# The two rope query tiles computed in the joined stage instead of the latent stage

## The chip, the cores and the metric

The kernel runs on one core of one Trainium2 chip. The metric is the device time of the whole program in microseconds (us), the median of several executions. One launch computes both layers for a prompt of 1024 tokens and for 8 samples of 16 tokens each, 1152 token columns in all.

## The reference

Every layer projects the normalised rows by `w_in` and splits the columns among four head groups. Only one of them, the latent attention (MLA), is touched here:

```
def _rope(x, pos):
    ...
    return jnp.concatenate([x1 * cos - x2 * sin, x2 * cos + x1 * sin], axis=-1)

def _mla(xq, xlat, xkr, pos, past_lat, past_kr, lat_g, w_uk, w_uv):
    q = xq.reshape(B, L, MLA_H, MLA_DN + MLA_DR)          # 4 heads, 64 + 32
    q = jnp.concatenate([q[..., :MLA_DN], _rope(q[..., MLA_DN:], pos)], axis=-1)
    lat = _rmsnorm(xlat, lat_g)
    kr = _rope(xkr, pos)
    ...
    scale = (MLA_DN + MLA_DR) ** -0.5
```

Beside it run a differential attention (4 heads with two score maps each), a gated chunk mixer (SGU) and a gated delta rule (GDN) whose inputs pass through a causal convolution of width 4.

## The kernel before

All arrays lie transposed, features on the 128 partitions and tokens along the row, in 3 blocks of 384 columns. A projection tile is 128 output features: 8 pieces of the contraction by 3 blocks. Operands are kept as a high and a low part, so one piece of one block is three matmuls with 384 columns (lines 264 to 266, `split_product`); this is called an item. A tile has 24 items. The weights of a tile are loaded by SP (`w_load`), rounded by ACT (`w_high`, line 251) and completed by POOL (`w_low`, line 259, a subtraction that reads and writes SBUF). Tiles are numbered through a layer, `GDN_W` to `MLA_W` and on, and three split slots turn round by this number.

A layer is a row of stages; at the end of each stage all engines meet. Those that matter here, in their order:

- `diff_stage`: queries and keys of the differential attention.
- `diff_gdn_stage`, the joined stage: the differential attention (32 turns: two head pairs, 8 query blocks `i` of 128 rows, two heads `e`) and dense projection items are woven on each engine by one list written out by hand, `fill`, which says how many items come after each step of the attention. A turn of block `i` works on `128*(i+1)` keys. On PE a turn holds its scores (line 1262), the transposes of the weights (line 1272, which wait for the DVE result of line 1352) and the values (line 1284). On DVE a turn is two bias additions and two maxima (lines 1339 and 1340), then after ACT's exponents lines 1349 to 1352. The first six of the dense tiles are GDN inputs, and their convolution runs on DVE: one multiplication (line 1378) and three multiply-adds (line 1380) over 1176 columns, at fixed places of the item count; below this is called a burst. Tiles 6 and 7 are the GDN gates, the last two (`JOIN_TILES = GDN_TILES + 2`) the MLA queries without position. These four are copied by ACT to `row` and kept in device memory by SP (line 1178).
- `sgu_stage`: the chunk mixer; it also loads the kept queries into `qT`.
- `mla_stage`, the latent stage: four tiles in the order `MLA_ORDER = (4, 5, 2, 3)`, that is the latent (LAT), the rope key (KR), the rope query (QR) and the same with its halves swapped (QS). ACT squares the latent, PE sums the squares (line 459), DVE and ACT turn the sums into a factor (lines 527 to 530), DVE ropes the key (lines 516 to 519) and the query (lines 534 to 543). SP writes the key and the latent row to the outputs and waits until both have landed before the stage can end.
- `expand_stage`: keys and values are expanded from the latent row by PE, ACT, DVE and POOL (line 786 on). Then comes the latent attention.

Of the kernel before, what the change touches and what calls it, by code (L numbers as in the profile page):

```python
# [11 lines left out]
P = 128  # L12
# [65 lines left out]
EARLY = 3  # L78
DQK_W, DV_AT, GDN_W, SV_AT, SU_AT, MLA_W, OUT_W, FFN_W = 0, 4, 6, 16, 18, 20, 24, 32
MLA_ORDER = (4, 5, 2, 3)  # L80
MLA_LATE = len(MLA_ORDER)
JOIN_TILES = GDN_TILES + 2
DIFF_ORDER = (2, 3, 0, 1)
# [19 lines left out]
def build(nc, d):  # L103
    top = ExitStack()
    with top:
# [63 lines left out]
        gate_keep = nc.dram_tensor("gate_keep", (P, 2, TOK), F32, kind="Internal").ap()  # L169
        qn_keep = nc.dram_tensor("qn_keep", (P, 2, TOK), F32, kind="Internal").ap()  # L170
        y_keep = nc.dram_tensor("y_keep", (P, 6, TOK), F32, kind="Internal").ap()
# [133 lines left out]
        def sgu_stage(l):  # L305
# [9 lines left out]
            with stage("sgu_par", "prod_ready", "freed_a", "sv_ready", "sv_freed", "vn_ready", "mix_ready", "mix_done",  # L315
# [3 lines left out]
                @block.sync  # L319
                def _(sp):  # L320
                    sp.dma_start(wsT[:, :, :, :], d["sgu_wT"][l]).then_inc(spar, 16)
                    sp.dma_start(ln[:, :, :], d["sgu_ln"][l]).then_inc(spar, 16)
                    sp.dma_start(sb[:, :, :, :], d["sgu_b"][l]).then_inc(spar, 16)
                    for n in range(SV_AT + 4, MLA_W + 4):
                        w_load(sp, l, n)
                    for hh in range(HEADS):
                        sp.dma_start(qT[0:64, hh, :], qn_keep[64 * (hh % 2):64 * (hh % 2) + 64, hh // 2, :]).then_inc(qnin, 16)
# [94 lines left out]
        def mla_stage(l):  # L422

            cosT = at("cosT", [P, TOK], R(24))
            sinT = at("sinT", [P, TOK], R(25))
            t1 = at("rope_t1", [P, NB, BLK], R(26))
            sq = at("lat_sq", [P, NB, BLK], R(27))
            tk = at("rope_tk", [64, BLK], R(35))
            LAT, KR, QR, QS = 0, 1, 2, 3
            own = lambda n: "V" if n in (KR, QR, QS) else "A"  # L430
            with stage("mla_aux", "prod_ready", "freed_a", "freed_v", "lat_sq_ready", "lat_sum", "lat_ready", "kr_ready",
                       "mla_link", "kv_out", "lat_recip", "lat_root") as (block, sems):
                (aux, ready, fa, fv, lsq, lsum, lready, krready, lnk, kvout, lrc, lrt) = sems
                freed = {"A": fa, "V": fv}

                @block.sync
                def _(sp):
                    for dst, src in ((cosT, "cos"), (sinT, "sin")):
                        sp.dma_start(dst[:, :], d[src]).then_inc(aux, 16)
                    for dst, src in ((wuk, "wuk"), (wuv, "wuv")):  # L440
                        sp.dma_start(dst[:, :], d[src][l]).then_inc(aux, 16)
# [21 lines left out]
                def _(pe):  # L463
                    for n in range(MLA_LATE):
                        pe.wait_ge(w_lod, MLA_W + n + 1)
                        slot = (MLA_W + n) % SSLOTS
                        for b in range(NB):
                            u = n * NB + b
                            cols = slice(b * BLK, (b + 1) * BLK)
                            if u >= 6:  # L470
                                who = own((u - 6) // NB)
                                pe.wait_ge(freed[who], sum(own(v // NB) == who for v in range(u - 5)))
                            for k in range(KD):
# [4 lines left out]
                        if n == KR:  # L478
                            lat_sums(pe, range(2))
                        if n == QR:  # L480
                            lat_sums(pe, range(2, NB))

# [6 lines left out]
                def _(act):  # L489
# [10 lines left out]
                    split(1)  # L500
                    split(2)
                    for b in range(NB):
                        if b == 2:
                            split(3)
                        act.wait_ge(lrc, b + 1)
                        act.sqrt(PS[:, 6 + b % 2, 0:BLK], PS[:, 6 + b % 2, 0:BLK]).then_inc(lrt, 1)

                @block.vector
                def _(dve):
                    scale = (MLA_DN + MLA_DR) ** -0.5  # L510
                    link = Link(dve, lnk)
                    dve.wait_ge(aux, 80)
                    for b in range(NB):
                        cols = slice(b * BLK, (b + 1) * BLK)
# [7 lines left out]
                    for b in range(NB):  # L522
# [14 lines left out]
                    for b in range(NB):  # L537
                        dve.wait_ge(ready, QS * NB + b + 1)
                        link(dve.scalar_tensor_tensor(out=bank(QS, b), in0=bank(QS, b), scalar=scale,
                                                      in1=sinT[:, b * BLK:(b + 1) * BLK], op0=ALU.mult,  # L540
                                                      op1=ALU.mult))
                        for hh in range(HEADS):
                            ins = dve.tensor_tensor(qT[64:96, hh, b * BLK:(b + 1) * BLK],
                                                    t1[32 * hh:32 * hh + 32, b, :],
                                                    bank(QS, b)[32 * hh:32 * hh + 32], ALU.add)
                        ins.then_inc(fv, 1)

# [548 lines left out]
        def diff_gdn_stage(l, bias):  # L1096
# [47 lines left out]
            with stage(*names) as (block, sems):  # L1144
# [4 lines left out]
                def _(sp):  # L1149
# [13 lines left out]
                    def projection():  # L1163
                        for t in range(ITEMS):
# [26 lines left out]
                    sp.wait_ge(acc_kept, 32 * 6)  # L1191
                    sp.wait_ge(row_kept[0], 32)
                    sp.wait_ge(row_kept[1], 32)

# [196 lines left out]
                def _(act):  # L1391
# [41 lines left out]
                    def projection():  # L1433
                        for t in range(ITEMS):
# [4 lines left out]
                            if j == 0 and 0 <= u < JOIN_TILES * NB:  # L1439
# [4 lines left out]
                                if b == 0 and n >= GDN_TILES:  # L1444
                                    act.wait_ge(row_kept[n % 2], 16)
# [1551 lines left out]
```

## Time and profile before

| what | value |
|---|---|
| median of 3 runs | 3513.42 us (3512.93 to 3527.26) |
| profiled execution, first to last instruction | 3513.3 us |
| PE busy | 3245.8 us (92%) |
| DVE busy | 2026.6 us (58%) |
| ACT busy | 902.5 us (26%) |
| POOL busy | 893.2 us (25%) |
| mean granted TensorE clock | 0.959 of 2.4 GHz |

The profiled execution is listed by its span, 3513.3 us; no other time of it is given, and the span lies 0.1 us under the median. A matmul's busy time counts its way through the array, so a PE that is shown busy is not a PE at its peak. The stages named above take, in the first layer, 134.8 to 348.8 us (joined), 348.8 to 412.1 (chunk mixer), 412.1 to 468.4 (latent) and 468.4 to 480.1 us (expand); the second layer repeats them 1725 us later.

### The profile page before, as it was taken

Reading aid. Unit: us, or ns where it says so; the run is one execution under the profiler, and the core shown is the slowest. Engines: PE = TensorE matmul, PEld = TensorE weight load, DVE = VectorE, ACT = ScalarE, POOL = GpSimd, SP = SyncE. Lnnn points to the kernel's source line nnn. Section 1 sums busy time; section 2 is a strip of 40 time slices with the busy share of each in tenths; the row PEclk is TensorE's granted clock in tenths of the full one; section 3 lists DMA queues with packets and bytes.
Section 4 is the critical chain, followed back from the end, with each engine's and each line's share of the span. In section 5 each row is a group of like instructions: output and inputs, shape, how many; then the busy total and the mean of one; then the engine's idle time right before and its main releaser. Section 6 shows DMA issues by size and latency. Waiting matters only on the chain. (4 is left out here: it accounts for less than half of the span.)

```text
span 3513.3 us, 57203 instructions
## 1 busy us (share of the span) xinstructions
PE 3245.8 (92%) x23900; PEld 3044.1 (87%) x23900; DVE 2026.6 (58%) x3500; ACT 902.5 (26%) x1650; POOL 893.2 (25%) x780
## 2 busy tenths in 40 slices
PE   5989988889999999999988999979899999999996
PEld 4978975779999999999978898648699999999996
DVE  7386454564555565555566755546627655555656
ACT  3244134233211111111233431532322111111112
POOL 2222120213322222222343211102133222222223
PEclk9999998799999999999999999979899999999998
DMA  5622231201111111111154212230011111111112
GB/s 211 194 88 95 90 115 41 82 18 37 41 43 43 43 42 37 49 37 43 35 179 151 94 70 91 95 115 9 23 43 41 49 37 37 49 43 43 42 43 71
DMA packets 122292, 237.42 MB, mean 68 GB/s; under 512 B 34084, under 2 KB 82980, under 8 KB 118632
## 3 DMA queue, kind: packets, MB, share of 16 engines
q1 hardware_dynamic: 122024, 233.65, 20.4%
q8 instruction: 192, 3.15, 0.4%
q14 instruction: 76, 0.62, 0.1%
HBM read 176.70 MB, written 56.54 MB: 66 GB/s over the span
## 5 line engine op out<-in xcount | busy, mean ns | idle before, releaser
L264 PE MATMUL PS<-h_split,w_split 128*128 128x384 f32 x3072 | 1064.9, 347 | 28.2 <-PEq L201 14.1
L266 PE MATMUL PS<-h_split,w_split 128*128 128x384 f32 x3072 | 1044.4, 340 | 0.0
L265 PE MATMUL PS<-h_split,w_split 128*128 128x384 f32 x3072 | 1040.1, 339 | 0.0
L259 POOL TENSOR_TENSOR w_split<-w_full,w_split 128x1024 fp32r<-128x1024 f32 (+1 forms) x194 | 476.6, 2457 | 963.5 <-ACT w_split L251 963.5
L264 PEld LDWEIGHTS PS<-h_split,w_split 128*128 128x128 f32 x3072 | 586.3, 191 | 47.5 <-issue 29.3
L265 PEld LDWEIGHTS PS<-h_split,w_split 128*128 128x128 f32 x3072 | 582.8, 190 | 2.5
L266 PEld LDWEIGHTS PS<-h_split,w_split 128*128 128x128 f32 x3072 | 582.3, 190 | 0.0
L251 ACT CAST w_split<-w_full 128x1024 fp32r<-128x1024 f32 (+1 forms) x194 | 202.0, 1053 | 1306.1 <-PE PS L266 1167.1
L2296 DVE TENSOR_TENSOR x<-x,PS 128x384 f32<-128x384 f32 x528 | 285.6, 552 | 178.5 <-PE PS L266 176.8
L264 PE MATMUL PS<-ffn_act,w_split 128*128 128x384 f32 x1056 | 367.7, 348 | 8.1 <-POOL w_split L259 7.1
L265 PE MATMUL PS<-ffn_act,w_split 128*128 128x384 f32 x1056 | 357.1, 338 | 0.0
L266 PE MATMUL PS<-ffn_act,w_split 128*128 128x384 f32 x1056 | 356.7, 338 | 0.0
L264 PEld LDWEIGHTS PS<-ffn_act,w_split 128*128 128x128 f32 x1056 | 199.4, 189 | 28.8 <-DVE x L2296 20.3
L2246 DVE TENSOR_TENSOR ffn_row<-PS,square_sums 128x384 f32<-128x384 f32 x176 | 93.3, 551 | 207.9 <-PE PS L266 205.6
L265 PEld LDWEIGHTS PS<-ffn_act,w_split 128*128 128x128 f32 x1056 | 199.5, 189 | 0.5
L266 PEld LDWEIGHTS PS<-ffn_act,w_split 128*128 128x128 f32 x1056 | 199.2, 189 | 0.0
L2267 DVE SCALAR_TENSOR_TENSOR ffn_gate<-ffn_row,par,ffn_gate 128x584 f32<-128x584 f32 x176 | 175.1, 1019 | 1.8
L2250 DVE TENSOR_TENSOR ffn_row<-PS,square_sums 128x256 f32<-128x256 f32 x88 | 37.4, 425 | 235.2 <-PE PS L266 235.2
L2267 DVE SCALAR_TENSOR_TENSOR ffn_up<-ffn_row,par,ffn_up 128x584 f32<-128x584 f32 x176 | 141.4, 843 | 3.0
L264 PE MATMUL PS<-o_hi,w_split 128*128 128x384 f32 x384 | 132.5, 345 | 10.7 <-DVE o_lo L1980 10.7
L2152 POOL COPY ffn_new<-ffn_row 128x2 f32<-128x2 f32 x88 | 17.5, 199 | 477.5 <-DVE ffn_row L2251 477.4
L1411 ACT ACTIVATE diff_P<-PS,diff_stat 128x128 f32<-128x128 f32 (+7 forms) x128 | 95.8, 748 | 148.3 <-DVE diff_stat L1340 148.2
(388 smaller groups left out, 4920.4 us busy)
## 6 DMA issues: line engine op xcount, KB each, us to landing
w_full<-in_w_up SPq DMA_DIRECT2D x88, 512.0 KB, 3.3
w_full<-in_w_down SPq DMA_DIRECT2D x44, 512.0 KB, 3.3
w_full<-in_w_in SPq DMA_DIRECT2D x38, 512.0 KB, 3.4
kq_keep<-split_rows SPq DMA_DIRECT2D x128, 128.0 KB, 2.4
kq_row<-kq_keep SPq DMA_DIRECT2D x32, 512.0 KB, 4.3
x<-x_keep SPq DMA_DIRECT2D x2, 4608.0 KB, 16.9
w_full<-in_w_out SPq DMA_DIRECT2D x16, 512.0 KB, 3.3
gdn_y<-y_keep SPq DMA_DIRECT2D x2, 3456.0 KB, 11.7
```

Source lines behind the costliest of these rows:

```text
L251: act.copy(ws[:, n % SSLOTS, 0, 0:w], wf[:, n % WSLOTS, 0:w]).then_inc(w_hid, 1)
L259: pool.tensor_tensor(ws[:, n % SSLOTS, 1, 0:w], wf[:, n % WSLOTS, 0:w], ws[:, n % SSLOTS, 0, 0:w].bitcast(F32), ALU.subtract).then_inc(w_l ...
L264: pe.matmul(out, w_hi, a_hi, start=first, stop=False)
L265: pe.matmul(out, w_hi, a_lo, start=False, stop=False)
L266: return pe.matmul(out, w_lo, a_hi, start=False, stop=last)
L1411: act.activation(Pb[:, v % 2, c, 0:n], S(c)[:, 0:n], ACT.Exp, bias=stat[:, 0, v, c:c + 1], accum_out=stat[:, 1, v, c:c + 1]).then_inc(p_do ...
L2152: pool.tensor_copy(new[:, t, 0:pad], row[:, SEQ:SEQ + pad])
L2246: dve.tensor_tensor(row[:, pad + b * BLK:pad + (b + 1) * BLK], src, ss[:, b, :], ALU.mult).then_inc(upf, 1)
L2250: dve.tensor_tensor(row[:, pad + 2 * BLK:pad + SEQ], src[:, 0:rest], ss[:, b, 0:rest], ALU.mult)
L2267: ins = dve.scalar_tensor_tensor(out=acc[:, a:b], in0=row[:, tap + a:tap + b], scalar=w(tap), in1=acc[:, a:b], op0=ALU.mult, op1=ALU.add)
L2296: dve.tensor_tensor(xs, xs, PS[:, 4 + u % 4, 0:BLK], ALU.add).then_inc(added, 1)
```

## The change

QR and QS leave the latent stage and become dense tiles 10 and 11 of the joined stage. There ACT scales and copies them like the other query tiles, and SP keeps all four in `q_keep`. The lists of the weave grow: the 16 turns of blocks 0 to 3 carry 9 items instead of 7, the 16 turns of blocks 4 to 7 carry 8 instead of 7, and 14 items remain behind the last turn as before. The latent stage loads the two kept rows into `rope_rows` behind cos and sin; DVE ropes the query from there before it touches the key. The swapping of weights into slots keeps its order, with the numbers of the tiles between moved by two.

```diff
-DQK_W, DV_AT, GDN_W, SV_AT, SU_AT, MLA_W, OUT_W, FFN_W = 0, 4, 6, 16, 18, 20, 24, 32
-MLA_ORDER = (4, 5, 2, 3)
+DQK_W, DV_AT, GDN_W, SV_AT, SU_AT, MLA_W, OUT_W, FFN_W = 0, 4, 6, 18, 20, 22, 24, 32
+MLA_ORDER = (4, 5)
-JOIN_TILES = GDN_TILES + 2
+JOIN_TILES = GDN_TILES + 4
...
+            qr = at("rope_rows", [P, 2, TOK], R(28))
...
                     for dst, src in ((cosT, "cos"), (sinT, "sin")):
                         sp.dma_start(dst[:, :], d[src]).then_inc(aux, 16)
+                    sp.dma_start(qr[:, :, :], q_keep[:, 2:4, :]).then_inc(rin, 16)
...
                         if n == KR:
-                            lat_sums(pe, range(2))
-                        if n == QR:
-                            lat_sums(pe, range(2, NB))
+                            lat_sums(pe, range(NB))
...
                     dve.wait_ge(aux, 80)
+                    dve.wait_ge(rin, 16)
+                    for b in range(NB):
+                        cols = slice(b * BLK, (b + 1) * BLK)
+                        dve.tensor_tensor(t1[:, b, :], qr[:, 0, cols], cosT[:, cols], ALU.mult)
+                        link(dve.tensor_tensor(qr[:, 1, cols], qr[:, 1, cols], sinT[:, cols], ALU.mult))
+                        for hh in range(HEADS):
+                            rows = slice(32 * hh, 32 * hh + 32)
+                            dve.tensor_tensor(qT[64:96, hh, cols], t1[rows, b, :], qr[rows, 1, cols], ALU.add)
...
-                    for b in range(NB):
-                        dve.wait_ge(ready, QR * NB + b + 1)
-                        dve.scalar_tensor_tensor(out=t1[:, b, :], in0=bank(QR, b), scalar=scale,
-                                                 in1=cosT[:, b * BLK:(b + 1) * BLK], op0=ALU.mult,
-                                                 op1=ALU.mult).then_inc(fv, 1)
...
-                fill += [3, 2, 2] if i < 4 else [2, 2, 2, 1]
+                fill += [3, 3, 3] if i < 4 else [2, 2, 2, 2]
...
-                                dst = gate_keep[:, n - 6, :] if n < GDN_TILES else qn_keep[:, n - GDN_TILES, :]
+                                dst = gate_keep[:, n - 6, :] if n < GDN_TILES else q_keep[:, n - GDN_TILES, :]
```

DVE in the joined stage, first head pair, the turn of query block 3 whose weights are 128x512 (`diff_P` is the weight row, `conv_acc` the convolution's sum). Before:

```order
L1352 SCALAR_TENSOR_TENSOR diff_P<-diff_P,diff_stat 128x512
L1339 TENSOR_TENSOR PS<-PS,bias_p_245 128x256
L1340 TENSOR_REDUCE diff_stat<-PS 128x1
L1339 TENSOR_TENSOR PS<-PS,bias_p_245 128x256
L1340 TENSOR_REDUCE diff_stat<-PS 128x1
L1349 RECIPROCAL diff_stat<-diff_stat 128x1
L1350 TENSOR_SCALAR diff_stat<-diff_stat,lam 128x1
L1352 SCALAR_TENSOR_TENSOR diff_P<-diff_P,diff_stat 128x512
```

The same place of the changed kernel:

```order
L1336 SCALAR_TENSOR_TENSOR diff_P<-diff_P,diff_stat 128x512
L1323 TENSOR_TENSOR PS<-PS,bias_p_245 128x256
L1324 TENSOR_REDUCE diff_stat<-PS 128x1
L1323 TENSOR_TENSOR PS<-PS,bias_p_245 128x256
L1324 TENSOR_REDUCE diff_stat<-PS 128x1
L1362 TENSOR_SCALAR conv_acc<-conv_row,par 128x1176
L1364 SCALAR_TENSOR_TENSOR conv_acc<-conv_row,par,conv_acc 128x1176 x3
L1333 RECIPROCAL diff_stat<-diff_stat 128x1
L1334 TENSOR_SCALAR diff_stat<-diff_stat,lam 128x1
L1336 SCALAR_TENSOR_TENSOR diff_P<-diff_P,diff_stat 128x512
```

The bursts stand at fixed item counts, so with more items in a turn they come in earlier turns. Before, one of the six fell whole into a turn (the first of block 4) and five were cut in two; now four fall whole into a turn (the first of block 3, the second of block 4, the first of block 6, the second of block 7) and two are cut.

DVE in the latent stage. Before, its last rows of the stage: the third block's norm, then the query's rope.

```order
L527 TENSOR_SCALAR PS<-PS 128x384
L528 RECIPROCAL PS<-PS 128x384
L530 SCALAR_TENSOR_TENSOR latT<-latT,par,PS 128x384
L534 SCALAR_TENSOR_TENSOR rope_t_4556<-PS,cosT 128x384 x3
L539 SCALAR_TENSOR_TENSOR PS<-PS,sinT 128x384
L543 TENSOR_TENSOR qT<-rope_t_4556,PS 32x384 x4
```

Now the query's rope opens the stage, three times the first three of these rows, and the key's rope follows; the norm rows come last:

```order
L507 TENSOR_TENSOR rope_t_4747<-rope_rows,cosT 128x384
L508 TENSOR_TENSOR rope_rows<-rope_rows,sinT 128x384
L511 TENSOR_TENSOR qT<-rope_t_4747,rope_rows 32x384 x4
L515 TENSOR_TENSOR rope_tk<-PS,cosT 32x384
L516 TENSOR_TENSOR rope_tk<-PS,sinT 32x384
L517 COPY PS<-rope_tk 32x384
L518 TENSOR_TENSOR krT<-rope_tk,PS 32x384
```

Moved ahead are 3 times 6 instructions, which now read SBUF alone where they read PSUM. PE at the end of the key tile, before:

```order
L264 MATMUL PS<-h_split,w_split 128x384
L265 MATMUL PS<-h_split,w_split 128x384
L266 MATMUL PS<-h_split,w_split 128x384
L459 MATMUL PS<-lat_sq,ones 128x384 x2
L264 MATMUL PS<-h_split,w_split 128x384
L265 MATMUL PS<-h_split,w_split 128x384
L266 MATMUL PS<-h_split,w_split 128x384
```

And now (line 740 is the first product of the expand stage):

```order
L264 MATMUL PS<-h_split,w_split 128x384
L265 MATMUL PS<-h_split,w_split 128x384
L266 MATMUL PS<-h_split,w_split 128x384
L459 MATMUL PS<-lat_sq,ones 128x384 x3
L207 UNCONDITIONAL_BRANCH
L736 UNCONDITIONAL_BRANCH
L740 MATMUL PS<-latT,wuk 128x512 x4
```

The 144 matmuls of QR and QS no longer stand between the sums and the end of the stage.

## Rows read from the trace of the kernel before

**Rows 1.** Timeline of one layer, SP and POOL: start us, us, engine, line, operation.
```profile
134.78 0.34 SPq L1181 DMA_DIRECT2D conv_old<-in_c_gconv  x1
...
348.81 0.35 SPq L321 DMA_DIRECT2D wsT<-in_sgu_wT  x1
...
412.11 0.35 SPq L439 DMA_DIRECT2D cosT<-in_cos  x1
...
468.43 2.01 POOL L786 COPY kT<-krT 32x1024 f32<-32x1024 f32 x2 [13.26 <-SPq L207]
...
480.14 0.54 SPq L2755 DMA_DIRECT2D o_diff<-dqT  x1
```

**Rows 2.** Timeline of PE in the latent stage: starts 18 items apart.
```profile
454.72 0.35 PE L264 MATMUL PS<-h_split,w_split 128*128 128x384 f32 x1
...
464.20 0.35 PE L264 MATMUL PS<-h_split,w_split 128*128 128x384 f32 x1
```

**Rows 3.** Groups of the joined stage, 137:347: busy, mean ns, idle before.
```profile
L1262 PE MATMUL PS<-k_stack,q_stack 128*128 128x512 f32 (+3 forms) x96 | 28.3, 351 | 4.4 <-POOL q_stack L567 2.6 <-ACT diff_P L1411 1.6
...
L1272 PE MATMUL PS<-cst,diff_P 128*128 128x128 f32 x144 | 25.0, 284 | 13.8 <-DVE diff_P L1352 9.2 <-ACT diff_PT_odd L1398 3.0 <-ACT diff_PT_even L1398 1.5
...
L1272 PEld LDWEIGHTS PS<-cst,diff_P 128*128 128x128 f32 x144 | 17.8, 144 | 19.9 <-DVE diff_P L1352 12.1 <-issue 7.0
```

**Rows 4.** Timeline of PE's weight loads in the joined stage, two long stalls.
```profile
203.74 0.71 PEld L1272 LDWEIGHTS PS<-cst,diff_P 128*128 128x128 f32 x4 [4.55 <-DVE diff_P L1352]
...
279.27 0.19 PEld L1262 LDWEIGHTS PS<-k_stack,q_stack 128*128 128x128 f32 x1 [2.91 <-POOL q_stack L567]
```

**Rows 5.** Timeline of DVE around a whole convolution burst.
```profile
191.95 0.88 DVE L1352 SCALAR_TENSOR_TENSOR diff_P<-diff_P,diff_stat 128x640 f32<-128x640 f32 x1
...
196.01 6.37 DVE L1380 SCALAR_TENSOR_TENSOR conv_acc<-conv_row,par,conv_acc 128x1176 f32<-128x1176 f32 x3
...
202.80 0.88 DVE L1352 SCALAR_TENSOR_TENSOR diff_P<-diff_P,diff_stat 128x640 f32<-128x640 f32 x1
```

**Rows 6.** Timeline of POOL and DVE: one operation beside POOL's and alone.
```profile
158.39 3.48 POOL L259 TENSOR_TENSOR w_split<-w_full,w_split 128x1024 fp32r<-128x1024 f32 x1
...
160.20 1.95 DVE L1352 SCALAR_TENSOR_TENSOR diff_P<-diff_P,diff_stat 128x256 f32<-128x256 f32 x1
...
165.51 0.49 DVE L1352 SCALAR_TENSOR_TENSOR diff_P<-diff_P,diff_stat 128x256 f32<-128x256 f32 x1
```

**Rows 7.** Windows: us, busy (x) of PE, PEld, DVE, ACT, POOL, PEclk, DMA.
```profile
200.00:210.00 10.00, 6.26 (x23) 5.80 (x24) 8.66 (x13) 3.00 (x7) 2.34 (x3) 0.66 0.53 164
```

**Rows 8.** Timeline of DVE in the latent stage.
```profile
437.71 0.55 DVE L516 TENSOR_TENSOR rope_tk<-PS,cosT 32x384 f32<-32x384 f32 x1 [1.94 <-PE PS L266]
...
440.31 0.57 DVE L527 TENSOR_SCALAR PS<-PS 128x384 f32<-128x384 f32 x1 [0.32 <-DVE krT L519]
...
452.29 0.57 DVE L527 TENSOR_SCALAR PS<-PS 128x384 f32<-128x384 f32 x1 [3.42 <-PE PS L459]
...
456.00 0.62 DVE L530 SCALAR_TENSOR_TENSOR latT<-latT,par,PS 128x384 f32<-128x384 f32 x1 [0.54 <-ACT PS L506]
...
465.53 2.25 DVE L543 TENSOR_TENSOR qT<-rope_t,PS 32x384 f32<-32x384 f32 x4
```

**Rows 9.** Groups of DVE in the latent stage, 411:469.
```profile
L543 DVE TENSOR_TENSOR qT<-rope_t,PS 32x384 f32<-32x384 f32 x12 | 6.6, 552 | 0.2
```

**Rows 10.** Timeline of SP: the latent row's output.
```profile
456.78 0.37 SPq L449 DMA_DIRECT2D out_o_lat<-latT  x1
```

**Rows 11.** DMA issues: KB each, median us to landing.
```profile
qn_keep<-conv_row SPq DMA_DIRECT2D x1, 576.0 KB, 2.8
...
sgu_keep<-suT SPq DMA_DIRECT2D x1, 1152.0 KB, 6.3
```

**Rows 12.** Timeline of PE at the expand stage, first and second layer.
```profile
468.46 5.37 PE L756 MATMUL PS<-latT,wuk 128*128 128x512 f32 x8 [3.57 <-PEq L201]
...
2194.05 3.67 PE L756 MATMUL PS<-latT,wuk 128*128 128x512 f32 x8 [3.58 <-PEq L201]
```

More of the change, by code:

```diff
@@ L169, in build @@
         gate_keep = nc.dram_tensor("gate_keep", (P, 2, TOK), F32, kind="Internal").ap()
-        qn_keep = nc.dram_tensor("qn_keep", (P, 2, TOK), F32, kind="Internal").ap()
+        q_keep = nc.dram_tensor("q_keep", (P, 4, TOK), F32, kind="Internal").ap()
         y_keep = nc.dram_tensor("y_keep", (P, 6, TOK), F32, kind="Internal").ap()
@@ L326, in _ @@
                     for hh in range(HEADS):
-                        sp.dma_start(qT[0:64, hh, :], qn_keep[64 * (hh % 2):64 * (hh % 2) + 64, hh // 2, :]).then_inc(qnin, 16)
+                        sp.dma_start(qT[0:64, hh, :], q_keep[64 * (hh % 2):64 * (hh % 2) + 64, hh // 2, :]).then_inc(qnin, 16)
                     sp.wait_ge(vnr, TT)
@@ L428, in mla_stage @@
             tk = at("rope_tk", [64, BLK], R(35))
-            LAT, KR, QR, QS = 0, 1, 2, 3
-            own = lambda n: "V" if n in (KR, QR, QS) else "A"
+            LAT, KR = 0, 1
             with stage("mla_aux", "prod_ready", "freed_a", "freed_v", "lat_sq_ready", "lat_sum", "lat_ready", "kr_ready",
-                       "mla_link", "kv_out", "lat_recip", "lat_root") as (block, sems):
-                (aux, ready, fa, fv, lsq, lsum, lready, krready, lnk, kvout, lrc, lrt) = sems
-                freed = {"A": fa, "V": fv}
+                       "mla_link", "kv_out", "lat_recip", "lat_root", "rows_in") as (block, sems):
+                (aux, ready, fa, fv, lsq, lsum, lready, krready, lnk, kvout, lrc, lrt, rin) = sems
                 @block.sync
@@ L469, in _ @@
                             cols = slice(b * BLK, (b + 1) * BLK)
-                            if u >= 6:
-                                who = own((u - 6) // NB)
-                                pe.wait_ge(freed[who], sum(own(v // NB) == who for v in range(u - 5)))
                             for k in range(KD):
@@ L500, in _ @@
                     split(1)
-                    split(2)
                     for b in range(NB):
-                        if b == 2:
-                            split(3)
                         act.wait_ge(lrc, b + 1)
@@ L509, in _ @@
                 def _(dve):
-                    scale = (MLA_DN + MLA_DR) ** -0.5
                     link = Link(dve, lnk)
                     dve.wait_ge(aux, 80)
+                    dve.wait_ge(rin, 16)
[6 more added lines that the diff above has]
+                            dve.tensor_tensor(qT[64:96, hh, cols], t1[rows, b, :], qr[rows, 1, cols], ALU.add)
                     for b in range(NB):
@@ L531, in _ @@
                                                  in1=s, op0=ALU.mult, op1=ALU.mult).then_inc(lready, 1)
-                    for b in range(NB):
-                        dve.wait_ge(ready, QR * NB + b + 1)
-                        dve.scalar_tensor_tensor(out=t1[:, b, :], in0=bank(QR, b), scalar=scale,
-                                                 in1=cosT[:, b * BLK:(b + 1) * BLK], op0=ALU.mult,
-                                                 op1=ALU.mult).then_inc(fv, 1)
[L537 to L546, printed above, removed]
         def keep_stacked(sp, n, halves, done):
@@ L1191, in _ @@
                     sp.wait_ge(acc_kept, 32 * 6)
-                    sp.wait_ge(row_kept[0], 32)
-                    sp.wait_ge(row_kept[1], 32)
+                    sp.wait_ge(row_kept[0], 16 * (JOIN_TILES - 6) // 2)
+                    sp.wait_ge(row_kept[1], 16 * (JOIN_TILES - 6) // 2)
                 @block.gpsimd
@@ L1444, in projection @@
                                 if b == 0 and n >= GDN_TILES:
-                                    act.wait_ge(row_kept[n % 2], 16)
+                                    act.wait_ge(row_kept[n % 2], 16 * ((n - 6) // 2))
                                 elif b == 0 and n >= 2:
```

## The prediction

> **What bounds the kernel now.** The page comes first: PE is busy for 92% of the span, so what counts is where PE is held up and what of its work can slide under somebody else's wait. The timeline of SP gives the stages [rows 1]: the joined stage lasts 348.81 - 134.78 = 214.0 us, the latent stage 468.43 - 412.11 = 56.3 us, the expand stage 480.14 - 468.43 = 11.7 us. The second layer repeats them, so every sum below is made for one layer and doubled.
>
> The groups of the joined stage show PE's idle time: 13.8 us ahead of the transposes, most of it until DVE's weight row (line 1352), and 4.4 us ahead of the scores, 18.2 us in all [rows 3]. Seen from the weight loads, 12.1 us in nine waits are for DVE [rows 3]. The longest, 4.55 us [rows 4], stands behind the one convolution burst that lies whole in a turn: from one weight row to the next DVE needs 202.80 - 191.95 = 10.85 us there, without a pause worth naming [rows 5]. After that wait the granted clock of the slice is 0.66 [rows 7], that is 6.8 of 10 us at 1.2 GHz, for 3.4 us of lost work. The next long wait, 2.91 us, is for POOL's copy of keys and queries, whose load SP had issued late [rows 4].
>
> The latent stage has dense matmuls from its start to 464.6, and DVE's chains are hidden beneath them: the key's rope (to about 440.0), the norm of blocks 0 and 1 and, after a wait of 3.42 us for PE's late sum, of block 2 (to 456.6) [rows 8]. The output of the latent row is issued at 456.78 [rows 10] and has 11 us to land before DVE ends at 467.8 [rows 8], so it costs nothing.
>
> **The change part by part.**
>
> *Work added to the joined stage.* 18 items take 464.20 - 454.72 = 9.48 us, 0.527 us each [rows 2]. Two tiles are 48 items: +25.3 us if nothing hides them.
>
> *What hides them.* Each turn now holds 1.05 us (blocks 0 to 3) or 0.53 us (blocks 4 to 7) more of PE's work, so each wait for DVE shrinks by that much, if DVE's share of the turn stays as it was. It doesn't quite: four bursts now lie whole in a turn instead of one. PE's mean turn was (214 - 32 items outside the turns x 0.527) / 32 = 6.2 us, and is 0.5 to 1.1 us longer now; DVE's burst turn is 10.85 us at block 4, less where rows are shorter, and DVE has some 2 us of lead to spend. That makes 2.3 us of wait at block 3, 3 us at block 4 (4.55 - 0.53 with POOL's subtraction in it, 2 without), 2 us at block 6, none at the second of block 7 (short rows follow), 0.8 us at the two cut ones. That is 8.1 instead of 12.1 us, -4.0. The wait for POOL's copy goes, since it came from SP standing behind a late burst and the bursts are now over before: -2.9. Waits for ACT's copies between transposes (4.5 us of the 13.8) have as many items between them as before and stay; for the small rest -1.0. One of two clock drops goes: half of 3.4, -1.7. The joined stage thus grows by 25.3 - 4.0 - 2.9 - 1.0 - 1.7 = **+15.7 us**. Bounds: all 18.2 us of idle time and the 3.4 us of clock come back, +3.7; nothing comes back, +25.3.
>
> The rest that moves there lies beside PE's 25 us: on SP two weight loads and two keeps, on ACT two casts and six copies, on POOL two subtractions (2.4 us each when alone). ACT and POOL are busy for a quarter of the span, so none is counted; if SP is late with a key load through them, it costs PE the 2.91 us of [rows 4] again, which a rival below takes up.
>
> *Work taken from the latent stage.* PE ends the key tile at 437.7, as before (DVE's first row behind it starts at 437.71 [rows 8]). Only the chain is left. DVE starts later than it could: it waits for cos, sin, the kept rows and three small loads, 2.75 MB. Before, the same number of bytes had landed with `sgu_keep`, issued at 416.4 and down 6.3 us later [rows 11], at 422.7; I take 422.3. The query's rope is 18 operations of about 0.552 us [rows 9] plus links, 10.3 us. In it falls POOL's subtraction at 427 (2.4 us). The rows show what that can do: the same multiply-add took 1.95 us beside POOL's subtraction and 0.49 us alone, and ended when POOL's did [rows 6]. So 0 to 2.4 us are added, I take 1.6. The query's rope ends at 434.2; the key's three blocks (2.3 us each) end at 441.1 to 441.6 instead of 440.0, 1.5 us late. One block of the norm takes 456.62 - 452.29 = 4.3 us [rows 8]; the third no longer waits for PE and follows at once, so the latent row is done at 440.31 + 3 x 4.3 + 1.5 = 454.7. SP issues its output 0.2 us later, alone on the queue now: 2.8 us, as `qn_keep` of the same size [rows 11]. Then 0.7 us to the next stage's first work, as between 467.8 and 468.43 [rows 1, 8]: the stage ends at 458.4 instead of 468.4, **-10.0 us**. So of 25.3 us taken from PE 15 are not won, because a DVE chain and one landing come out from under it. Bounds: -11.6 (DVE never late) and -7 (loads down at 424.5 and a full hold).
>
> On DVE's hold the Trainium skill (SBUF — State Buffer, section on the two separate sides) says that a DVE operation with two SBUF inputs and a GpSimd operation that reads SBUF exclude each other for the whole instruction, whoever starts first. The old rope read PSUM and was free of it; the new one falls under it. By that rule the hold is either the rest of 2.4 us or, if DVE comes first, none for DVE, and my sum moves by -1.6 or +0.8 us a layer.
>
> *The expand stage.* PE idles for 20 us before it instead of 3.6. In the first layer its first eight rows took 5.37 us with a clock drop, in the second 3.67 us without [rows 12], and both stages last 11.7 us, since POOL sets the end. So one short drop is free; a longer one costs some: **+0.7 us**, from 0 to about 4.8, an estimate for the case that the 3.67 us and the products behind them, as many again, all run at half rate, less the time that POOL needs anyway.
>
> *Sum.* 15.7 - 10.0 + 0.7 = +6.4 us a layer, +12.8 us for both: 3513.3 + 12.8 = **3526 us**. The profiled span is within 0.1 us of the median, so no correction is needed. It is 0.4% slower, within 0.5%, which is about what a measurement of this kernel can tell from no change.
>
> **The rivals.**
>
> *The joined stage takes it all in.* If DVE's backlog clears, the bursts' waits vanish: +3.7 - 9.3 = -5.6 a layer, 3502 us. For it speaks that no burst is left for the second head pair, against it that a whole burst outlasts PE's turn by some 4 us. Faster by over 0.5% needs still more, joined growth under 0.5 us. Chance 0.12 for about 3502, half of it below 3496.
>
> *The bursts and SP cost as much as they free (slower).* Place: the turns of blocks 4 and 6. If two of the whole bursts each bring the 4.55 us seen at the one of before, with a clock drop of 3.4 us each, and SP's two more ordered waits make one load late again, the growth stays at 25 us: +25 - 9.3 = +15.7 a layer, 3545 us. It decides from a joined growth of 18.1 us on, where the total passes 0.5%. For it: DVE's 10.85 us against PE's 6.7 to 7.3. Chance 0.27.
>
> *The latent stage comes back colder and later.* Loads down at 424.5, a full hold and 4.8 us in the expand stage: 15.7 - 7 + 4.8 = 13.5 a layer, 3540 us. Chance 0.09. The Trainium skill (TensorE: Matmul & The Clock Gate, section on the clock gate) says that the throttled clock is the default and activity releases it; by that rule 20 us of idling makes the drop certain in both layers, where the rows show it in one of two. A certain short drop changes nothing in the sum.
>
> **How the numbers follow.** The forecast (3515 to 3536) has 0.52, the full intake 0.12, the busy bursts 0.27, the cold stage 0.09. Of the forecast's own share a fifth lies above 3531. Slower by over 0.5% (3531): 0.1 + 0.24 + 0.06 = about 0.38; faster 0.07; within 0.5% the rest, 0.55. The range from 3504 to 3545 leaves out some 0.08 below and 0.1 above.
>
> **What the changed profile would show.** The joined stage at about 230 us (218 or 239 by the rivals); waits for DVE of about 8 us, longest at blocks 3, 4 and 6; none for POOL's copy. In the latent stage DVE's rope from about 422, one of its rows stretched to some 2 us; PE idle for 20 us; the output of the latent row issued at about 42.7 us after the stage's start and landed 3 us later. I am wrong if the joined stage is off by more than 5 us, or if something other than this landing ends the latent stage.

## The result, and the profile after

| kernel | median, us | from to, us | runs | against before |
|---|---|---|---|---|
| before | 3516.13 | 3510.25 to 3527.26 | 22 | |
| changed | 3524.86 | 3516.8 to 3537.28 | 22 | 1.0022, 95% interval 1.0014 to 1.003 |

The change costs 0.22%, some 9 us, and lies within 0.5%. The forecast was 3526 us, +12.8 over its own base; its base of 3513.3 us lies 2.8 us under the median of the 22 runs. The stage boundaries on SP come first, as in [rows 1]; they are those of the changed kernel, first layer, and then the second layer's:

```profile
135.03 0.34 SPq L1165 DMA_DIRECT2D conv_old<-in_c_gconv  x1
...
361.11 0.35 SPq L321 DMA_DIRECT2D wsT<-in_sgu_wT  x1
...
424.43 0.35 SPq L438 DMA_DIRECT2D cosT<-in_cos  x1
...
472.21 2.99 POOL L770 COPY kT<-krT 32x1024 f32<-32x1024 f32 x3 [27.36 <-SPq L207]
...
484.16 0.54 SPq L2739 DMA_DIRECT2D o_diff<-dqT  x1
...
1864.20 0.34 SPq L1165 DMA_DIRECT2D conv_old<-in_c_gconv  x1
...
2089.71 0.35 SPq L321 DMA_DIRECT2D wsT<-in_sgu_wT  x1
...
2152.98 0.35 SPq L438 DMA_DIRECT2D cosT<-in_cos  x1
...
2202.20 5.33 PE L740 MATMUL PS<-latT,wuk 128*128 128x512 f32 x8 [10.49 <-PEq L201]
...
2213.88 0.53 SPq L2739 DMA_DIRECT2D o_diff<-dqT  x1
```

Of the kernel before, [rows 1] has the first layer; two more of its second layer are:

```profile
2136.15 0.35 SPq L439 DMA_DIRECT2D cosT<-in_cos  x1
...
2205.73 0.54 SPq L2755 DMA_DIRECT2D o_diff<-dqT  x1
```

Differences of these starts give the lengths (an expand stage ends with `o_diff`):

| stage, us | before, layers 1 and 2 | changed | difference |
|---|---|---|---|
| joined | 214.0, 212.1 | 226.1, 225.5 | +12.1, +13.4 |
| chunk mixer | 63.3, 63.3 | 63.3, 63.3 | 0 |
| latent | 56.3, 57.9 | 47.8, 49.2 | -8.5, -8.7 |
| expand | 11.7, 11.7 | 11.9, 11.7 | +0.2, 0 |

They sum to +8.5 us, the 8.7 us between the medians. The two profiled spans are further apart, 3526.5 and 3513.3: the 4.7 us more lie nearly all in stages that the change does not touch, behind the second expand stage (1312.6 us against 1307.6). In the profiles of the experiments below that same stretch takes 1304 to 1313 us, so stages are compared here, not spans. A stage too is not the same from profile to profile: four kernels below keep the joined stage of the changed kernel as it is, and there it takes 224.2 to 228.6 us, 226.3 in the mean of their eight. So the growth of the joined stage is known to some 2 us.

The groups of PE in the changed joined stage, 137:352, answer to [rows 3]; the columns are the same. The window ends before the last 8 of the 144 transposes; up to the end of the stage, the wait for DVE is the same 8.0 us:

```profile
L1246 PE MATMUL PS<-k_stack,q_stack 128*128 128x512 f32 (+3 forms) x96 | 27.4, 341 | 2.4 <-POOL q_stack L551 1.4 <-ACT diff_P L1395 1.1
L1256 PE MATMUL PS<-cst,diff_P 128*128 128x128 f32 x136 | 22.7, 274 | 9.4 <-DVE diff_P L1336 6.5 <-ACT diff_PT_odd L1382 1.7 <-ACT diff_PT_even L1382 1.2
...
L1256 PEld LDWEIGHTS PS<-cst,diff_P 128*128 128x128 f32 x136 | 16.8, 140 | 12.9 <-DVE diff_P L1336 8.0 <-issue 3.8
```

The weight loads' wait for DVE fell from 12.1 to 8.0 us in five waits. The longest of them, and the one for POOL's copy:

```profile
163.72 0.20 PEld L1256 LDWEIGHTS PS<-cst,diff_P 128*128 128x128 f32 x2 [1.22 <-DVE diff_P L1336]
...
194.40 0.42 PEld L1256 LDWEIGHTS PS<-cst,diff_P 128*128 128x128 f32 x4 [1.37 <-DVE diff_P L1336]
...
204.76 0.30 PEld L1246 LDWEIGHTS PS<-k_stack,q_stack 128*128 128x128 f32 x2 [1.68 <-POOL q_stack L551]
...
217.29 0.42 PEld L1256 LDWEIGHTS PS<-cst,diff_P 128*128 128x128 f32 x4 [2.89 <-DVE diff_P L1336]
...
239.82 0.42 PEld L1256 LDWEIGHTS PS<-cst,diff_P 128*128 128x128 f32 x4 [2.28 <-DVE diff_P L1336]
```

The whole joined stage as one window (us, busy and count of PE, PEld, DVE, ACT, POOL, granted clock), before and then changed, first and second layer each:

```profile
134.78:348.81 214.03, 192.77 (x1249) 176.11 (x1250) 150.86 (x249) 96.72 (x240) 59.31 (x62) 0.96 0.31 103
1860.77:2072.83 212.06, 192.00 (x1249) 176.14 (x1250) 148.84 (x249) 96.82 (x240) 59.50 (x62) 0.96 0.31 104
```

```profile
135.03:361.11 226.08, 211.11 (x1393) 198.20 (x1394) 152.25 (x249) 100.70 (x248) 64.95 (x64) 0.99 0.32 108
1864.20:2089.71 225.51, 211.51 (x1393) 198.47 (x1393) 152.23 (x249) 100.80 (x248) 65.03 (x64) 0.98 0.32 108
```

PE's idle time is the length less the busy time: 21.3 us before, 15.0 after, -6.3 (second layer 20.1 and 14.0). The time lost to the clock is estimated as the length times what the clock lacks to 1: 0.04 x 214 = 8.6 before, 0.01 x 226 = 2.3 after (second layer 8.5 and 4.5). The clock is given in hundredths, so each of these is good to about 1 us. The same sum over windows of 10 us gives 8.1 before and 2.7 after, and 8.5 and 3.5 in the second layer. Of these, 3.0 and 2.7 (1.7 and 1.7 in the second layer) are lost in the first 10 us of the stage, in both kernels.

DVE and POOL in the changed latent stage, against [rows 8]:

```profile
435.97 0.56 DVE L507 TENSOR_TENSOR rope_t<-rope_rows,cosT 128x384 f32<-128x384 f32 x1 [12.16 <-DMA wukT<-in_wukT]
...
442.61 2.66 DVE L507 TENSOR_TENSOR rope_t<-rope_rows,cosT 128x384 f32<-128x384 f32 x1
...
448.03 0.55 DVE L515 TENSOR_TENSOR rope_tk<-PS,cosT 32x384 f32<-32x384 f32 x1
...
455.65 0.57 DVE L526 TENSOR_SCALAR PS<-PS 128x384 f32<-128x384 f32 x1 [0.32 <-DVE krT L518]
...
467.83 0.61 DVE L529 SCALAR_TENSOR_TENSOR latT<-latT,par,PS 128x384 f32<-128x384 f32 x1 [0.54 <-ACT PS L498]
```

```profile
442.05 2.80 POOL L259 TENSOR_TENSOR w_split<-w_full,w_split 128x1024 fp32r<-128x1024 f32 x1 [14.11 <-ACT w_split L251]
```

DVE stands until the last small load has landed, 11.5 us into the stage (12.9 in the second layer), then works through without a gap worth naming to 468.44: query, key, norm. One query row began 0.56 us behind POOL's subtraction and ended 0.42 us behind it; it took 2.66 us instead of 0.56. The latent row's output is issued 44.2 us into the stage and the next stage begins 3.6 us after it.

### The profile page after: what moved, and what is told of

Same layout as the page of the kernel before. It is cut to its first block and busy times, and to the rows that moved or that the text cites. A ratio compares the mean times of both kernels' runs of the same rounds, so it can differ in the third digit from the quotient of the medians.

```text
span 3526.5 us, 57213 instructions
## 1 busy us (share of the span) xinstructions
PE 3245.1 (92%) x23900; PEld 3044.9 (86%) x23900; DVE 2034.9 (58%) x3500; ACT 906.3 (26%) x1662; POOL 894.2 (25%) x780
## 5 line engine op out<-in xcount | busy, mean ns | idle before, releaser
L259 POOL TENSOR_TENSOR w_split<-w_full,w_split 128x1024 fp32r<-128x1024 f32 x194 | 478.9, 2469 | 976.0 <-ACT w_split L251 976.0
L264 PEld LDWEIGHTS PS<-h_split,w_split 128*128 128x128 f32 x3072 | 584.3, 190 | 47.8 <-issue 29.8
L251 ACT CAST w_split<-w_full 128x1024 fp32r<-128x1024 f32 x194 | 201.9, 1052 | 1277.6 <-PE PS L266 1138.4
```

Of the source, the lines that this page charges most:

```text
L251: act.copy(ws[:, n % SSLOTS, 0, 0:w], wf[:, n % WSLOTS, 0:w]).then_inc(w_hid, 1)
L259: pool.tensor_tensor(ws[:, n % SSLOTS, 1, 0:w], wf[:, n % WSLOTS, 0:w], ws[:, n % SSLOTS, 0, 0:w].bitcast(F32), ALU.subtract).then_inc(w_l ...
L264: pe.matmul(out, w_hi, a_hi, start=first, stop=False)
```

## The experiments

Each ran beside the kernel before on one chip. Ratios are to that kernel, whose median there was 3519 to 3521 us and not 3516; so ratios are compared, and not times.

**All new items behind the last turn.**

```diff
-                fill += [3, 3, 3] if i < 4 else [2, 2, 2, 2]
+                fill += [3, 2, 2] if i < 4 else [2, 2, 2, 1]
```

> The changed kernel with the old weave (7 items in every turn), so that the 48 items of the two tiles stand behind the last turn. Theory: these items are worth their 25.3 us of PE a layer, and only their place inside the turns hides part of it. Then the joined stage lasts 214 + 25 = 239 us instead of 226, PE's waits for DVE are back at some 12 us in nine, and the program is about 25 us slower than the changed kernel, 3550 us, 1.0% over the kernel before. Rival: DVE bounds the joined stage, so that it doesn't matter where PE's items stand; then the stage stays at about 226 us and the program at 3525.

Measured: 3550.78 us, ratio 1.0089 (1.0061 to 1.0117). The joined stage takes 236.8 and 240.5 us, 10.7 and 14.9 more than in the changed kernel; the weight loads wait 10.7 us for DVE:

```profile
L1256 PEld LDWEIGHTS PS<-cst,diff_P 128*128 128x128 f32 x144 | 17.7, 142 | 18.2 <-DVE diff_P L1336 10.7 <-issue 6.6
```

Against the kernel before, the stage is 22.8 and 28.4 us longer, 25.6 in the mean. So the 25 us of items are full price where nothing covers them, and the places in the turns earn back about half. That is what the changed lists are worth.

**The bursts spread.** The four convolution operations of a tile stand 5 items apart instead of 2, the store of the result 7 items later.

```diff
-                            n, j = divmod(t - 36, TILE_ITEMS)
+                            n, j = divmod(t - 43, TILE_ITEMS)
...
-                            if 0 <= n < 6 and j % 2 == 0 and j // 2 < GDN_TAPS:
-                                j //= 2
+                            if 0 <= n < 6 and j % 5 == 0 and j // 5 < GDN_TAPS:
+                                j //= 5
```

> The changed kernel with the four convolution operations of a tile five items apart instead of two (and the output of its sum issued seven items later), so that none of the six bursts lies whole in a turn. Theory: the 8 us of waits for DVE's weight rows come from whole bursts; they fall to 2 to 3 us, the joined stage from 226 to about 220 us, the program by 8 to 12 us to about 3515, level with the kernel before. Rival: the waits come from the chain of exponents on ACT and would be there without bursts; then they stay at 8 us and nothing moves by more than 2 us.

Measured: 3504.62 us, ratio 0.9952 (0.9934 to 0.997). Groups of its joined stage, 137:352, and the stage as windows:

```profile
L1246 PE MATMUL PS<-k_stack,q_stack 128*128 128x512 f32 (+3 forms) x96 | 27.3, 340 | 2.0 <-ACT diff_P L1395 1.1 <-POOL q_stack L551 0.9
L1256 PE MATMUL PS<-cst,diff_P 128*128 128x128 f32 x144 | 23.6, 273 | 2.1 <-ACT diff_PT_odd L1382 1.3 <-ACT diff_PT_even L1382 0.8
```

```profile
134.74:351.61 216.87, 209.24 (x1393) 197.64 (x1394) 147.98 (x249) 101.01 (x248) 59.20 (x64) 0.99 0.33 112
1862.24:2078.36 216.12, 209.20 (x1393) 197.62 (x1394) 147.13 (x249) 101.01 (x248) 59.45 (x64) 0.99 0.33 112
```

No wait for DVE is left in the groups, with the same DVE work, and idle time falls from 15.0 to 7.6 us. The stage is 9.2 and 9.4 us shorter. This is the length that my rival of full intake named (+3.7 over before; measured +2.8 and +4.1). What had kept the change from it is the lump of the bursts and nothing about the amount of work. The gain is larger than expected (about 220 us and 3515). The store had to move with the operations; its own share is not separated here, but the weight loads' wait for POOL's copy fell only from 1.7 to 1.2 us. Three later kernels with the same spread have joined stages of 215.7 to 217.5 us.

**The same spread on the kernel before**, to tell whether the room came from the change.

> The kernel before, with its own lists of the weave and its latent stage of four tiles, and the four convolution operations of a tile spread over 5 items each instead of 2. Theory (the lump alone makes the waits): the 12.1 us of waits for DVE and the clock drops behind them go here as well, the joined stage shrinks from 214.0 and 212.1 to about 201, the program by about 24 us, to about 3493; moving the two tiles is then worth nothing by itself. Rival (the two moved tiles made the room in which the spread operations fit): with 7 items in a turn DVE is still late on average, some 6 us of waits stay, the joined stage is 207 or more and the program 3505 or more, no faster than the changed kernel with the same spread.

Measured: 3502.69 us, ratio 0.9946 (0.9931 to 0.9962); joined stage 202.5 and 203.9 us. Groups of its weight loads, 137:343:

```profile
L1272 PEld LDWEIGHTS PS<-cst,diff_P 128*128 128x128 f32 x144 | 17.7, 140 | 10.7 <-issue 5.8 <-DVE diff_P L1352 3.9
L1262 PEld LDWEIGHTS PS<-k_stack,q_stack 128*128 128x128 f32 x96 | 17.6, 188 | 8.1 <-POOL q_stack L567 6.6 <-ACT diff_P L1411 1.2 <-issue 0.3
```

It lies between the two theories: the joined stage nearer to the first (201), the program's time nearer to the rival (3505). The wait for DVE falls from 12.1 to 3.9 us, not to none, so the 7 items of a turn seem a little short; and the wait for POOL's copy grows from 2.9 to 6.6 us. Against the changed kernel with the same spread the joined stage is 14.4 and 12.2 us shorter and the latent and expand stages together 9.6 and 8.2 us longer: moving the tiles costs some 4 to 5 us a layer with or without the lump. That is read from the stages of one profile of each kernel; the ratios, 0.9946 and 0.9952, cannot tell it from nothing.

**SP's store asked for 3 items later**, on that kernel (`t - 46` instead of `t - 43`).

> The kernel before with the convolution operations spread over 5 items, and SP's store of a finished convolution row asked for 3 items later, so that SP doesn't stand behind DVE with a load of keys and queries queued after it. Theory (the 6.6 us of waits for POOL's copy that the spread brought come from SP waiting for the later last operation): they fall under 3 us, the joined stage goes from 202.5 and 203.9 to about 199, the program from 3502.7 to about 3495. Rival (the load is late by its own place in the order, or DVE then waits for the stored row): the joined stage stays at 202 or more and the program within 3 us of 3502.7.

Measured: 3501.47 us, ratio 0.9946 (0.9933 to 0.9959), joined stage 200.6 and 201.0 us. A row of its waits (who, for whom, us in all, times, the longest):

```profile
PEld PS L1262 <- POOL q_stack L567: 3.1, 1, 3.1
```

The wait for POOL's copy halves, and the stage shortens by 1.9 and 2.9 us, no more than a stage differs between profiles. SP standing behind DVE was half of that wait. The program's time stayed within 3 us of 3502.7, as the rival had it, and not at 3495; so the wait is explained, but its worth is not shown.

**The kept rows loaded in the chunk mixer**, so that DVE waits only for cos and sin.

```diff
+                    sp.dma_start(qr[:, :, :], q_keep[:, 2:4, :]).then_inc(qnin, 16)
                     sp.wait_ge(vnr, TT)
...
-                        sp.dma_start(dst[:, :], d[src]).then_inc(aux, 16)
-                    sp.dma_start(qr[:, :, :], q_keep[:, 2:4, :]).then_inc(rin, 16)
+                        sp.dma_start(dst[:, :], d[src]).then_inc(rin, 16)
...
-                    dve.wait_ge(aux, 80)
-                    dve.wait_ge(rin, 16)
+                    dve.wait_ge(rin, 32)
```

> The changed kernel with the kept query rows loaded during the chunk mixer stage into free rows, and DVE in the latent stage waiting for cos and sin alone instead of all five loads and the rows. Theory: DVE's late start (11.5 and 12.9 us into the stage) is what makes the latent stage's chain late; it starts at about 6 us, the key's rope ends right behind PE (27 to 28 us in), and the latent stage falls by 3 to 4 us a layer to about 44.5, the program by 6 to 8 us to about 3518. Rival: POOL's subtraction and PE's clock set the chain; then DVE starts earlier, waits for PE at the key and the stage falls by less than 1 us.

Measured: 3520.45 us, ratio 1.0003 (0.9989 to 1.0018). DVE in its second and in its first layer:

```profile
2159.52 0.56 DVE L506 TENSOR_TENSOR rope_t<-rope_rows,cosT 128x384 f32<-128x384 f32 x1 [7.95 <-DMA sinT<-in_sin]
```

```profile
444.91 0.55 DVE L514 TENSOR_TENSOR rope_tk<-PS,cosT 32x384 f32<-32x384 f32 x1 [2.86 <-PE PS L270]
...
449.12 0.55 DVE L514 TENSOR_TENSOR rope_tk<-PS,cosT 32x384 f32<-32x384 f32 x1 [1.94 <-PE PS L270]
```

DVE starts 7.3 us into the second layer's stage instead of 12.9, but the key's rope then waits for PE's key tile, and the latent stage gains 1.4 and 1.7 us only (46.4 and 47.5). It is between the theory (3 to 4 us) and the rival (under 1). The late loads were worth that much and no more: right behind them stands PE.

**The landing of the outputs awaited one stage later.** SP waits for both latent outputs in the expand stage (a semaphore `lat_out` that outlives the stage) instead of in the latent stage.

> The changed kernel in which the outputs of latent row and rope key are awaited at the end of the expand stage instead of the latent stage. Theory: the landing of the latent row ends the latent stage (3.6 us from its issue to the next stage, of which 0.7 us are the change of stages); the stage falls by 2.8 us a layer to 45, the program by some 5.5 us to 3519. Rival: PE's cold clock takes it back, since the expand stage begins 3 us sooner but lasts longer; then the expand stage grows by 2 us or more and less than 2 us are won in all.

Measured: 3520.54 us, ratio 1.0000 (0.9985 to 1.0015). PE's first row of the expand stage comes 45.7 us after the latent stage's start in both layers, against 47.8 and 49.2; output issue to next stage is now 1.3 us instead of 3.6:

```profile
468.94 0.37 SPq L449 DMA_DIRECT2D out_o_lat<-latT  x1
...
470.24 5.68 PE L743 MATMUL PS<-latT,wuk 128*128 128x512 f32 x8 [8.16 <-PEq L201]
```

So 2.3 us of the chain were the landing, a layer. The expand stage stays at 11.7 us, so the rival's slower clock takes nothing back.

**The norm first.** PE sums the squares of a block behind the next block, DVE makes the norm, then the key's rope, the query's last; the latent row's output is issued before the key's.

```diff
-                        if n == KR:
-                            lat_sums(pe, range(NB))
+                            if 1 <= u <= NB:
+                                lat_sums(pe, [u - 1])
```

> The changed kernel; in the latent stage the sums of squares follow each block, DVE makes the norm first, then the key's rope, and the query's rope last, so that the latent row's output lands under DVE's work. Theory (the stage's end is DVE's chain plus one landing): the 2.8 us of landing and the wait of 11.5 us before DVE's first row come out of the chain, the latent stage falls from 47.8 and 49.2 to about 42, the program by about 12 us, to about 3513. Rival (something else, PE or the other loads, ends the stage): it stays above 46 and the program at 3520 or more.

Measured: 3512.88 us, ratio 0.9982 (0.9972 to 0.9991). Timelines of DVE, and of SP and PE:

```profile
434.49 0.57 DVE L513 TENSOR_SCALAR PS<-PS 128x384 f32<-128x384 f32 x1 [11.56 <-PE PS L459]
...
456.00 0.56 DVE L531 TENSOR_TENSOR rope_t<-rope_rows,cosT 128x384 f32<-128x384 f32 x1 [0.24 <-DVE krT L526]
...
463.70 2.24 DVE L535 TENSOR_TENSOR qT<-rope_t,rope_rows 32x384 f32<-32x384 f32 x4
```

```profile
448.70 0.36 SPq L447 DMA_DIRECT2D out_o_lat<-latT  x1
...
466.61 6.63 PE L745 MATMUL PS<-latT,wuk 128*128 128x512 f32 x8 [14.01 <-PEq L201]
```

The latent stage is 466.61 - 423.55 = 43.1 us (44.1 in the second layer), 4.7 and 5.1 less. The output now lands under the query's rope, and the rope itself takes 9.9 us without a stretched row, since POOL's subtraction now falls elsewhere; so the gain holds both, the landing and some 2 us of that row. DVE still begins only 10.9 us into the stage, now for PE's first sum.

**Two blocks of the query's rope in the expand stage**, on top of that.

> As the one with the norm first, and blocks 1 and 2 of the query's rope move on DVE into the expand stage, where POOL sets the end. Theory: the latent stage is about 35 us, the expand stage 12 to 13, both together 48 instead of 59.7 and 60.9, the program by about 24 us less than the changed kernel, about 3501. Rival (DVE is late for its copies in the expand stage and that stage grows by what the other lost): both together 54 or more, the program 3512 or more.

Measured: 3504.26 us, ratio 0.9958 (0.9944 to 0.9972). DVE and PE in its expand stage:

```profile
458.86 1.42 DVE L768 TENSOR_TENSOR rope_t<-rope_rows,cosT 128x384 f32<-128x384 f32 x1 [0.68 <-PEq L205]
```

```profile
469.40 3.02 PE L750 MATMUL PS<-wuv,latT 128*128 128x256 f32 x8 [2.89 <-DVE val L775]
```

The latent stage is 36.4 us as expected, but the expand stage grows to 15.1 us: beside POOL's copies one of the first block's rows takes 1.42 us instead of 0.56, and PE waits 2.89 us for DVE's late copy of the values. Both together are 51.5 and 50.1 us, between the two expectations.

**Both edits together**, the spread and that one.

> The two edits together on the changed kernel: the convolution operations spread over 5 items each, the norm first and two blocks of the query's rope in the expand stage. If the two causes are independent, as both theories have it: joined stage 217, latent and expand stage together 48, some 21 us less than the changed kernel in each layer, about 3482. Rival (the clock or the later stages take part back): 3492 or more.

Measured: 3489.38 us, ratio 0.9904 (0.9889 to 0.992). Joined 216.9 and 217.5 us, latent and expand 51.5 and 50.5. Stage by stage the two edits add up; most of what is missing to 3482 is the growth of the expand stage, by 3.4 and 2.4 us here, seen in the kernel above.

**The rope in the chunk mixer.** With the spread and the norm first, the query's rope stands between the token tiles of the chunk mixer.

```diff
+                        if 2 <= t < 8:
+                            b, half = divmod(t - 2, 2)
...
+                            if half == 0:
+                                dve.tensor_tensor(t1[:, b, :], qr[:, 0, cols], cosT[:, cols], ALU.mult)
...
+                            for hh in ((0,) if half == 0 else (1, 2, 3)):
```

> The changed kernel with the convolution operations spread over 5 items, the norm first in the latent stage, and the whole rope of the query moved into the chunk mixer: two or four operations of 0.55 us after each of six token tiles, where DVE waits 1.73 us for PE at each tile. Theory: the chunk mixer stays at 63.3 us, the latent stage is about 36 (the key's rope, one landing, the change of stage), the expand stage 11.8, the joined stage 217; the program about 3482. Rival (DVE holds up PE in the chunk mixer, or the loads of cos, sin and the rows come too late there): the chunk mixer grows beyond 66 us and the program stays above 3487.

Measured: 3482.25 us, ratio 0.9887 (0.9871 to 0.9903). DVE there, and PE at the next change of stage:

```profile
364.25 0.56 DVE L405 TENSOR_TENSOR rope_t<-rope_rows,cos_early 128x384 f32<-128x384 f32 x1 [0.44 <-DMA sin_early<-in_sin]
...
367.09 1.68 DVE L409 TENSOR_TENSOR qT<-rope_t,rope_rows 32x384 f32<-32x384 f32 x3
```

```profile
450.83 6.48 PE L753 MATMUL PS<-latT,wuk 128*128 128x512 f32 x8 [6.34 <-PEq L201]
```

That is the time expected. The chunk mixer takes 64.1 and 64.6 us, 0.8 and 1.3 more than before and short of the rival's 66; the latent stage takes 35.4, latent and expand together 47.1 and 47.2 us instead of 59.7 and 60.9. **With the landing awaited in the expand stage as well:**

> The same, and the landing of the two latent outputs is awaited in the expand stage instead of the latent stage. Theory: the latent stage ends 0.7 us behind the key's rope, at about 33 us, 2.5 us less in each layer than with the landing awaited; the program 5 us less, about 3477. Rival (something else ends the stage then, the small loads or PE): latent and expand stage together stay above 46.5 us.

Measured: 3478.89 us, ratio 0.988 (0.9864 to 0.9895), latent and expand together 45.5 us in both layers. It is the fastest version: 1.2% under the kernel before. Beside the kernel before with the spread and the later store, on the same chip, it is 22.6 us faster, so with a cover for its chain the move pays. That compares the fastest tried of each: the norm first was not tried on the kernel before, whose latent stage has its chains under PE.

## Why the prediction was right, step by step

*The sum.* +6.4 us a layer was forecast, +3.8 (12.1 - 8.5 + 0.2) and +4.7 were measured. The direction, the two big terms and their bounds held; the joined stage was over-priced by 2.3 to 3.6 us, the latent gain by 1.3 to 1.5, and these two misses cancel in part. That 3526 lies only 1.1 us from the measured 3524.86 is luck: the growth was 8.7 us and not 12.8, and the base had been 2.8 us too low. By its own signs the forecast stands: the joined stage is 3.9 and 4.5 us off the 230, under the 5 allowed but not by much, and the landing ends the latent stage. One sum in the chances is off: 0.1 + 0.24 + 0.06 is 0.40, not 0.38.

*The waits for DVE.* 8.1 us forecast, 8.0 measured. The places were right as well: the whole burst in block 3 made the wait of 1.37 us at 194.40 (2.3 forecast), the one behind the second row of block 4 made 2.89 (3), that of block 6 2.28 (2), that of block 7 none (none) and the first cut one 1.22 (0.8 for both). The 4.55 us of [rows 4] are gone.

*POOL's copy.* Forecast to go, but 1.7 us stay at 204.76, behind a key load that SP issued late again (at 195.30, behind its store of a convolution). Of the 2.9 us counted 1.2 were won. The later-store run shows the same queue.

*The rest and the clock.* Forecast -1.0 and -1.7. Idle time fell by 6.3 us in all, 1.6 less than the 7.9 of my three terms. The clock gave back more than the 1.7: 6.3 and 4.0 us by the stage's mean, 5.4 and 5.0 by windows of 10 us. That is the mis-sized term: I counted one drop in [rows 7], where the windows before show more of them:

```profile
274.00:284.00 10.00, 7.41 (x35) 6.82 (x34) 4.91 (x11) 3.05 (x9) 2.27 (x4) 0.84 0.58 187
1920.00:1930.00 10.00, 5.77 (x30) 5.36 (x29) 9.75 (x11) 3.04 (x7) 3.52 (x1) 0.80 0.35 113
```

Each stood at one of the waits that went or shrank, so a shorter wait can be paid twice, once in idle time and once in clock. It isn't always: behind the changed kernel's wait of 2.9 us in block 5 the clock stays at 1.00 in the first layer and is 0.83 over 10 us in the second.

*The added work.* 48 x 0.527 = 25.3 us. With the spread, where the clock is 0.99 in both kernels in the first layer, PE's busy time grows by 209.24 - 186.31 = 22.9 us, 0.478 an item. The first layer of the kernel before with the spread, as a window:

```profile
134.83:337.33 202.50, 186.31 (x1249) 171.76 (x1249) 145.72 (x249) 97.00 (x240) 54.67 (x62) 0.99 0.32 109
```

This does not show a cheaper item: by the weight loads of the same two windows the growth is 197.64 - 171.76 = 25.9 us, 0.539 an item, and the run with all items last paid 25.6 us. How much counts as busy and how much as idle depends on which of PE's two rows is read; the lengths agree with the forecast's price.

*The latent stage.* -10.0 forecast, -8.5 and -8.7 measured. I took the first layer for both, but the stage before was 57.9 us in the second layer, not 56.3. The start of DVE was taken at 10.2 us and was 11.5 and 12.9. I had put the landings in one row with `sgu_keep` [rows 11]; the wait was for the last small load. The stretched row cost 2.1 and 2.2 us, not 1.6: the Trainium skill (SBUF — State Buffer, section on the two separate sides) says that of two such operations the one that starts first has the ports for its whole instruction, and the trace agrees: the row ended 0.42 us behind POOL's. Landing and change of stage took 3.6 us, forecast 3.5. That the landing, and not PE, ends the stage was right, and the run that awaits the landing later shows it.

*The expand stage.* +0.7 forecast, +0.2 and 0 measured, although the clock was at half for some 20 us and the first eight rows took 6.73 and 5.33 us instead of 5.37 and 3.67 [rows 12]. In the second layer POOL still sets its end, with four copies and four fills (`MEMSET`) up to 2213.22 us; in the first DVE's last copy ends at 483.54, 0.28 us behind POOL.

*The rivals.* Full intake did not happen, and the spread run shows that only the lump forbade it. The costly bursts did not happen either: no wait of 4.55 us came back. Of the colder and later latent stage, half came: DVE began 11.5 and 12.9 us into the stage, about as late as that rival had it (12.4), and the hold was full; but the slow clock, which came in both layers, cost 0.2 us at most in the expand stage instead of 4.8.

## What to carry to other kernels

Work moved under waits is worth what the waits give, so look first at what makes them: here spreading four DVE operations won about twice what the move cost, on either kernel. Taking work away from PE saves time only down to the chain that lay beneath it; before moving matmuls, time that chain alone, with its last load and its last landing, and give it another cover. An output that nobody reads in the next stage need not be awaited at the end of this one.

## What the hardware showed that I had not expected

PE's last dense row in the changed latent stage ends at about 454. From about 458 the granted clock is at its lower level, 1.2 GHz, for some 20 us; of these, this is a part (window as above):

```profile
460.00:470.00 10.00, 1.62 (x2) 0.50 (x2) 7.29 (x6) 0.95 (x2) 0.00 (x0) 0.50 0.05 22
```

PE has two matmuls to do in it, and the slow clock cost nothing there and nearly nothing in the expand stage, where POOL, or DVE's last copy 0.3 us behind it, is the bound. DVE's rows of two SBUF inputs are stretched by POOL's copies too, not only by its subtraction: 1.42 us instead of 0.56 in the expand stage, beside 32x1024 copies.
